# Inverse root of the query and key norms in a second attention: a root on ScalarE and a reciprocal, or eleven VectorE steps

## The reference, cut to what matters

```python
def rms_norm(x, g):
    xf = x.astype(jnp.float32)
    y = xf * lax.rsqrt(jnp.mean(xf * xf, axis=-1, keepdims=True) + EPS)
    return (y * g.astype(jnp.float32)).astype(x.dtype)
...
    q = rms_norm(q.reshape(bsz, s_len, ATTN_HEADS, HEAD_DIM), q_norm_g[i])
    k = rms_norm(k.reshape(bsz, s_len, ATTN_HEADS, HEAD_DIM), k_norm_g[i])
    v = v.reshape(bsz, s_len, ATTN_HEADS, HEAD_DIM)
    y_b = stick_breaking_attention(q, k, v).reshape(bsz, s_len, ATTN_W)
```

## Time and profile before

| | |
|---|---|
| time, median of 3 runs | 2665.98 us (2664.98 to 2666.3) |
| profiled execution, own time | 2665.14 us |
| its span, first to last instruction | 2663.3 us |
| PE busy | 2636.1 us, 99% of the span |
| DVE busy | 1966.9 us, 74% |
| ACT busy | 1130.1 us, 42% |
| POOL busy | 1340.2 us, 50% |

### The profile page before, as it was taken

One profiled execution on the slowest core, in us unless ns is written; L12 is line 12 of the kernel. 1 busy time (PEld: TensorE's weight loads), 2 busy tenths in 40 slices (PEclk: granted clock), 3 DMA queues, 4 the chain that ended last, 5 costly groups with the idle time before them and its releaser, 6 DMA issues.

```text
span 2663.3 us, 38109 instructions
## 1 busy us (share of the span) xinstructions
PE 2636.1 (99%) x14606; PEld 2127.9 (80%) x14606; DVE 1966.9 (74%) x2329; ACT 1130.1 (42%) x1650; POOL 1340.2 (50%) x868
## 2 busy tenths in 40 slices
PE   8999999999999999999999999999999999999999
PEld 6888877887788888888888666678878888888887
DVE  7777687777767676687689688855875657777775
ACT  6555533444443333344454355532343334443451
POOL 3111100002477777798845322132577777888842
PEclk9999999999999999999999999999999999999999
DMA  4111011112123332455422111112134445544412
GB/s 142 26 44 45 25 48 47 43 56 81 48 85 110 111 111 84 162 169 159 135 64 95 41 41 41 41 41 110 44 107 160 145 160 189 177 150 152 153 60 79
DMA packets 103711, 251.54 MB, mean 94 GB/s; under 512 B 10952, under 2 KB 15024, under 8 KB 100080
## 3 DMA queue, kind: packets, MB, share of 16 engines
q1 hardware_dynamic: 98576, 234.90, 27.1%
q10 hardware_dynamic: 4960, 14.27, 1.4%
HBM read 188.40 MB, written 58.11 MB: 93 GB/s over the span
## 4 chain that ended last, share of the span: by engine, by line
PE 91%; DVE 4%; ACT 2%; POOL 1%; issue 1%; DMA 1%; SPq 0%; ACTq 0%; DVEq 0%; POOLq 0%
PE ps L1234 10%; PE ps L1236 9%; PE ps L1235 9%; PE ps L1370 9%; PE ps L1372 8%; PE ps L1371 8%; PE ps L1418 6%; PE ps L1420 6%; PE ps L1419 6%; PE ps L1594 2%; PE ps L1819 1%; PE ps L1843 1%; PE ps L1829 1%; PE ps L1582 1%; PE ps L1568 1%; PE ps L1571 1%
## 5 line engine op out<-in xcount | busy, mean ns | idle before, releaser
L1234 PE MATMUL ps<-a_hi,w_hi 128*128 128x512 f32 x1100 | 454.5, 413 | 3.6 <-DVE a_lo L2095 2.2
L1236 PE MATMUL ps<-a_hi,w_lo 128*128 128x512 f32 x1100 | 431.1, 392 | 0.0
L1235 PE MATMUL ps<-a_lo,w_hi 128*128 128x512 f32 x1100 | 429.7, 391 | 0.0
L1088 POOL TENSOR_TENSOR w_lo<-w_raw,w_hi 128x512 fp32r<-128x512 f32 x212 | 289.3, 1366 | 118.3 <-ACT w_hi L2965 118.2
L1035 POOL TENSOR_TENSOR w_hi<-w_raw,der 128x1024 fp32r<-128x1024 f32 x44 | 83.7, 1903 | 523.1 <-PE ps L1236 476.4
L2965 ACT ACTIVATE w_hi<-w_raw 128x512 fp32r<-128x512 f32 (+1 forms) x259 | 176.3, 682 | 358.4 <-PE ps L1372 187.9
L2561 DVE TENSOR_TENSOR x<-ps,x 128x512 f32<-128x512 f32 x356 | 236.4, 687 | 31.9 <-PE ps L1420 31.9
L1088 POOL TENSOR_TENSOR w_lo<-asum,w_hi 128x512 fp32r<-128x512 f32 x151 | 209.0, 1384 | 87.1 <-ACT w_hi L2965 87.1
L1234 PEld LDWEIGHTS ps<-a_hi,w_hi 128*128 128x128 f32 x1100 | 207.5, 189 | 50.3 <-issue 7.6
L1236 PEld LDWEIGHTS ps<-a_hi,w_lo 128*128 128x128 f32 x1100 | 206.6, 188 | 45.6
L1235 PEld LDWEIGHTS ps<-a_lo,w_hi 128*128 128x128 f32 x1100 | 207.7, 189 | 34.3
(11 more groups left out here) (492 smaller groups left out, 6818.5 us busy)
## 6 DMA issues: line engine op xcount, KB each, us to landing
fb_wait<-hidden SPq DMA_DIRECT2D x56, 512.0 KB, 3.8
w_raw<-in_w_mix SPq DMA_DIRECT2D x54, 512.0 KB, 3.5
hidden<-hcomb SPq DMA_DIRECT2D x27, 1024.0 KB, 3.9
w_raw<-in_w_f SPq DMA_DIRECT2D x96, 256.0 KB, 3.2
w_raw<-in_w_gu SPq DMA_DIRECT2D x88, 256.0 KB, 2.6
fa_wait<-hidden SPq DMA_DIRECT2D x28, 512.0 KB, 3.9
hidden<-hbuf SPq DMA_DIRECT2D x27, 512.0 KB, 5.6
w_raw<-in_w_ple SPq DMA_DIRECT2D x16, 512.0 KB, 3.5
```

The costliest lines, as they stand in the source:

```text
L1088: nc.gpsimd.tensor_tensor(ring(w_lo, r), src, ring(w_hi, r).bitcast(F32), ALU.subtract).then_inc(e_lo, 1)
L1234: mm(ps[:, bank, :], wh, hi[:, k, cols], start=(n == 0), stop=False)
L1235: mm(ps[:, bank, :], wh, lo[:, k, cols], start=False, stop=False)
L1236: last = mm(ps[:, bank, :], wl, hi[:, k, cols], start=False, stop=(n == nk - 1))
```

## The change

For queries and keys the root on ACT is dropped, at all four places. In `head_factor` DVE makes the inverse root itself. It takes the bits of the mean as an integer, shifts them right by one, subtracts them from the constant 0x5f3759df, and so has a first guess `y`. Three Newton steps follow, each of which squares `y`, multiplies by the mean, and corrects `y`. In all these are eleven instructions on 128 x 256 elements, each waiting for the one ahead of it. The first of them raises the semaphore `st_root` that ACT raised before. The mean stays where it is, and so do the places in DVE's order. The gated branch (`N_SG`) keeps its root on ACT and its reciprocal. Two new tiles of 1 KB a partition hold the guess and a trial value.

```diff
         hsm = at("hsm", T // 4, S0 + 57 * KB)
+        guess = at("guess", T // 4, S0 + 58 * KB)
+        trial = at("trial", T // 4, S0 + 59 * KB)
...
             def head_factor(n):
 
+                if n == N_SG:
+                    dve.wait_ge(st_root, n + 1)
+                    nc.vector.reciprocal(hsm[:, :], hsm[:, :]).then_inc(st_inv, 1)
+                    return
+                dve.wait_ge(st_var, n + 1)
+                v, y, t = hsm[:, :], guess[:, :], trial[:, :]
+                ts(y.bitcast(I32), v.bitcast(I32), 1, None, ALU.logical_shift_right).then_inc(st_root, 1)
                 dve.wait_ge(st_root, n + 1)
-                nc.vector.reciprocal(hsm[:, :], hsm[:, :]).then_inc(st_inv, 1)
+                step(ts(y.bitcast(I32), y.bitcast(I32), -1, 0x5f3759df, ALU.mult, ALU.add))
+                for n_ in range(3):
+                    step(stt(t, y, -0.5, y, ALU.mult, ALU.mult))
+                    step(tt(t, t, v, ALU.mult))
+                    if n_ < 2:
+                        step(stt(y, t, 1.5, y, ALU.add, ALU.mult))
+                stt(v, t, 1.5, y, ALU.add, ALU.mult).then_inc(st_inv, 1)
...
                     av(rstd_f[:, :], banks(2), ACT.Copy).then_inc(xf_ready, 1)
-                    head_sqrt(N_QK)
                     act.wait_ge(x_out, 16 * KT)
...
                         if n == 4:
                             square(p + 1, 0)
-                        elif n == 7:
-                            head_sqrt(N_QK + p + 1)
```

## The result

| | before | after |
|---|---|---|
| time, median of 11 runs each, on one chip | 2665.98 us | 2673.44 us |
| lowest and highest | 2664.79 to 2667.79 | 2671.8 to 2675.88 |
| ratio, 95% interval | | 1.0027 [1.0019, 1.0034] |
| profiled execution, own time | 2665.14 us | 2673.44 us |

The change costs 7.5 us, 0.27%. The forecast was 2672.3 us.

The account below looks back on a forecast made before the run. PE, busy 99%, loses time only where it stands still; DVE, not ACT, closes each pair. 2.53 us ahead of the first pair plus 3.78 in three pairs gives +6.3: 2672.3 us against the median, range 2667.0 to 2675.5.

Parts of the forecast that it names:

- The chain: DVE's eleven dependent instructions at each of four places: 4.73 us, or 4.97 with integers at 0.42.
- The rival of the short chain: Dependent instructions follow as fast as independent ones, semaphores costing nothing: 3.58 us at each place, 2667.7 us in all; chance 0.18.
- The first pair: Ahead of the first pair PE only waits, so DVE's longer work delays everything behind it: +2.53 us.
- The pairs: Within each of three pairs DVE starts segment 8's scans 2.42 us late, of which 1.26 remain at the end: +3.78 us.
- its two waits: DVE's waits from segment 8 to a pair's end, 0.27 and 0.73 us, saved with 0.08 us more at each.
- ACT's relief is spent: Within a pair PE stops waiting some 0.9 us for ACT's copies, but waits for DVE's segment 8 weights instead.
- PE's clock: Rival: ahead of the first pair, 3.1 us of idleness lowers the clock, losing 2.1 us: 2674.4 us; chance 0.13.
- nearer the one that did no harm: PE's 3.1 us idleness ahead of the first pair was placed closer to 2.17 us, after which matmuls ran at full rate.
- the two cases that the prediction set 3.1 us between: Earlier PE idleness: 7.34 us at the start, then 0.63 us matmuls; 2.17 us, then 0.40 us matmuls at 2.4 GHz.
- The relief as a rival: With at most 2.57 us of DVE steps, each pair keeps the 0.9 us PE waits for ACT: 2663.7 us; chance 0.07.
- Edits at nothing: Factors' store and spread loads stay hidden though 2.5 us later; POOL's work, `st_root`, new tiles and gated branch cost 0.
- moves along: Ahead of the first pair POOL's work starts behind PE's, so it shifts with it at no cost.

Follow-up runs that it names:

- relief_only: Kernel before, with ACT's root within the three pairs replaced by a plain copy (computes something else, only a gauge): 2662.92 us, 0.9988.
- fill_dummy: Changed kernel with twelve 512-column matmuls, their result overwritten, put into PE's idle time ahead of the first pair's spread: 2670.62 us, 1.0019 against before.
- fill_one: Changed kernel with one k-step of PE's projection (three matmuls) moved from behind the first pair's spread to ahead of it: 2672.68 us, 1.0025 against before.
- mixed_cubic: Changed kernel, but first pair keeps root and reciprocal and later pairs take six DVE instructions with one third-order step, less accurate: 2662.75 us, 0.9988 against before.
- mixed_two: Changed kernel, but first pair keeps root and reciprocal and the three later pairs take two Newton steps instead of three: 2665.3 us, 0.9997 against before.
- fill_first: Changed kernel with the last two k-steps of PE's projection (six matmuls) moved ahead of the first pair's spread: 2678.78 us, 1.0049 against before.
- fill_gated: `fill_first` with POOL's weight splits of unit `U_SB + 4` held back until the factors are ready: 2672.45 us, 1.0024 against before.
- two_steps: Changed kernel with two Newton steps instead of three at all four places, the last step's accuracy left out: 2666.33 us, 1.0001 against before.
- first_only: Changed kernel with the eleven steps only ahead of the first pair; the three later pairs keep root and reciprocal: 2669.18 us, 1.0014 against before.

## Why the prediction came out as it did

**The chain.** Predicted 4.73 us, measured 4.75 ahead of the first pair. The integers take 0.29 where 0.30 was taken, the nine others 0.42, and the starts lie 0.46 apart. The rival of the short chain needed 0.34 and is out. What it had wrong is not the price of a semaphore: the product of the earlier trace rows that is followed after 0.34 us raises one too (`sw_ready`). What costs 0.12 us is that the next instruction waits for the one ahead. The Trainium skill, page "VectorE: DVE Perf Modes", section "The DRAIN you can't avoid", says that a semaphore behind each of eight copies costs nothing extra over one behind the last. The prediction held this to be the rival; read as the price of raising a semaphore, these rows do not contradict it.

**The first pair.** Predicted +2.53, measured +2.56 us for the chain itself.

**The pairs.** Predicted +1.26, measured +1.04. Behind the mean the scan of segment 8 is 2.44 us late (predicted 2.42), the products at 1550.80 are 2.08 late, so the first wait gave back 0.36 (0.35 predicted), and the instruction at 1554.23 starts 2.25 us behind the start of the scan ahead of it where it was 3.07, so the second wait gave back 0.82 (0.81 predicted). The term that was mis-sized is what DVE saves on the way, put at "its two waits". There was a third, small pause: before, the scan behind the products of the earlier trace rows started at 1544.94, 0.07 us behind their end, while the one at 1551.98 starts 0.09 us ahead of it. These 0.16 us, and 0.02 in the products themselves, are nearly all of the difference of 0.22.

**"ACT's relief is spent".** Right for the end of a pair, but the relief was larger than it looked: `relief_only` puts it at 1.1 us, not at the 0.35 of one wait or the 0.9 of another. The chain costs 4.67 us of DVE up to the scan (1544.54 - 1539.87) where the reciprocal without its wait costs 1.67 (1538.72 - 1537.05): 3.00 us more. Of these 0.74 + 0.09 vanish in DVE's wait ahead of segment 10 and 1.1 are paid by the relief, which leaves 1.07.

**PE's clock.** This is the step that failed. The prediction put 3.1 us of idleness "nearer the one that did no harm", and gave the fall a chance of 0.13. In the profiled execution it fell, at a price of 1.73 us (2.1 predicted). The sum of the forecast without it would have been 2.56 + 3.13 = 5.7 us against 6.3 predicted; with it, it is 7.4. So it is in part luck that the forecast of 2672.3 us came within 1.2 us: the three pairs were put 0.65 us too high, and the clock's 1.73 us were not in the sum. `fill_dummy`, which takes only the idleness away, has 4.8, and `fill_one` shows a fall after 2.45 us.

Neither of the two cases that the prediction set 3.1 us between was a good guide. The 2.17 us that did no harm lie close to gaps that do: in all twelve profiled executions PE stands still at this place, near 16.4 us, for 1.42 to 2.17 us in five, whose clock stays at 1.00, and for 2.65 to 2.83 us in seven, whose clock is 0.50 to 0.52 from 18 to 20 us. And for the 7.34 us at the start the lower level was read from the matmuls' 0.63 us alone: the windows of before give a granted clock of 1.00 from 7 to 12 us.

How often the changed kernel pays the 1.73 us is not shown run by run, since a run without a profile gives only its mean clock, and that falls with the gap near 16.4 us too (0.95 and 0.96 in the first two stretches of 20 us of `relief_only`).

**The relief as a rival.** Its condition, a chain of at most 2.57 us, held where it was tried: `mixed_cubic` with 2.46 keeps the whole relief, 1.1 us a pair where 0.9 was put down, and `mixed_two` with 1539.90 + 0.42 - 1536.95 = 3.37 keeps 0.3.

**Edits at nothing.** The spread transfers are hidden as predicted. That POOL "moves along" ahead of the first pair held too, but `fill_first` shows what that cover is worth: 2.00 + 2.44 - 2 x 0.42 = 3.6 us on DVE once POOL's release comes ahead of the spread.

## What to carry to other kernels

Count a chain of dependent VectorE instructions by its start-to-start time, and ask at each place separately what it delays: here the same eleven instructions cost 2.56 us where TensorE stood waiting and 1.04 where a loop had slack and ScalarE was relieved in return. When a chain leaves TensorE idle, add the price of its lower clock behind the gap; here it fell behind gaps of 1.7 to 3.1 us, most times though not always. Before work is moved to fill such a gap, look at what its end releases on other engines.

## What the runs showed of the hardware beyond that

- TensorE's granted clock fell to 0.50 after 2.45 us (`fill_one`) and 3.13 us (changed kernel) of standing still, and to 0.50 again behind a second gap of 2.58 us (`fill_gated`) and of 1.70 us (`fill_one`). It stayed at 1.00 after 1.76 us (`two_steps`) and, in one execution, after 3.14 us (`first_only`). The length of the gap alone does not decide it; what else does stays open.
- A VectorE instruction on two tensors grew from 0.42 to 2.00 and 2.44 us beside a GpSimd product of 1.91 and 2.40 us.
- Integer shift and multiply-add on 128 x 256 elements take 0.29 us, where a product of that size takes 0.42.
